# Expert activations turned by VectorE in 32 by 32 squares instead of by TensorE

## What is computed

```python
def expert_choice_ffn(h, w_router, w_gate, w_up, w_down):
    B, S, D = h.shape
    T = B * S
    xt = h.reshape(T, D)
    aff = jax.nn.softmax(jnp.einsum('td,de->te', xt, w_router).astype(jnp.float32), axis=-1)
    cap = CAPACITY_FACTOR * T // N_EXPERTS
    g, idx = lax.top_k(aff.T, cap)
    xe = xt[idx]
    hid = jax.nn.silu(jnp.einsum('ecd,edf->ecf', xe, w_gate)) * jnp.einsum('ecd,edf->ecf', xe, w_up)
    ye = jnp.einsum('ecf,efd->ecd', hid, w_down) * g[..., None].astype(h.dtype)
    out = jnp.zeros_like(xt).at[idx.reshape(-1)].add(ye.reshape(-1, D))
    return out.reshape(B, S, D)
```

## Time and profile before

| | us |
|---|---|
| median of 3 runs | 2111.11 |
| lowest, highest | 2111.06, 2111.87 |
| profiled execution | 2112.38 |
| its span, first to last instruction | 2110.5 |
| TensorE busy in the span | 1996.5 (95%) |
| VectorE, ScalarE, GpSimd busy | 399.8, 289.6, 138.5 |
| mean granted TensorE clock | 0.978 of full speed |
| moved by DMA | 639 MB, mean 303 GB/s |

### The profile page before, as it was taken

How to read it: one execution, slowest core, us unless ns; L and a number is a source line. 1 busy time by engine, 2 the same in 40 slices (tenths; PEclk the granted TensorE clock), 3 DMA queues, 4 the chain that set the end, 5 groups by cost and what they waited for, 6 DMA issues and landing times.

```text
span 2110.5 us, 37578 instructions
## 1 busy us (share of the span) xinstructions
PE 1996.5 (95%) x17115; PEld 921.3 (44%) x17115; DVE 399.8 (19%) x745; ACT 289.6 (14%) x556; POOL 138.5 (7%) x197
## 2 busy tenths in 40 slices
PE   6999999999957999999999999999999999999993
PEld 3888777776742333333333333333333333333331
DVE  1432255544360000010000100001000001000002
ACT  4222244442210000000000000000000000000001
POOL 1000000000100000010000100000000000100003
PEclk9999999999968999999999999999999999999997
DMA  9651111113059999999999999999999999999963
GB/s 381 234 203 58 33 56 50 41 51 130 30 213 374 393 395 413 389 385 408 389 411 389 399 393 389 410 391 407 395 381 413 388 412 389 381 412 389 414 222 106
DMA packets 101816, 639.19 MB, mean 303 GB/s; under 512 B 11489, under 2 KB 14945, under 8 KB 44065
## 3 DMA queue, kind: packets, MB, share of 16 engines
q1 hardware_dynamic: 95120, 620.32, 73.5%
q0 software_dynamic: 6544, 16.52, 3.7%
HBM read 622.90 MB, written 13.89 MB: 302 GB/s over the span
## 4 chain that ended last, share of the span: by engine, by line
PE 91%; DVE 3%; DMA 2%; ACT 2%; issue 1%; POOL 1%; SPq 0%; POOLq 0%; DVEq 0%; ACTq 0%
PE ps L738 87%; DMA slab_x<-in_w_mod_blocks 1%; PE ps L1122 1%; PE ps L907 1%; DVE negm L1614 1%; PE ps L1167 1%; PE ps L1125 0%; DMA xe<-xn_dram,idx_g 0%; DVE gq_lo L1586 0%; DVE in_lo L1538 0%; ACT in_hi L1233 0%; ACT gq_hi L1287 0%; DVE topi L1751 0%; PE ps L1038 0%; PE ps L826 0%
## 5 line engine op out<-in xcount | busy, mean ns | idle before, releaser
L738 PE MATMUL ps<-ring,xeT 128*32 128x512 f32 (+1 forms) x9216 | 927.2, 558 | 5.3 <-DVE hid L1832 3.3
L738 PEld LDWEIGHTS ps<-ring,xeT 128*32 128x32 f32 x9216 | 293.8, 110 | 601.7 <-issue 595.3
L738 PE MATMUL ps<-ring,hidT 128*32 128x512 f32 x4224 | 465.1, 592 | 0.9 <-ACT hidT L1442 0.9
L738 PEld LDWEIGHTS ps<-ring,hidT 128*32 128x32 f32 x4224 | 135.8, 110 | 305.2 <-issue 302.8
L1832 DVE TENSOR_TENSOR hid<-sil,ps 128x768 f32<-128x768 f32 (+1 forms) x48 | 42.6, 888 | 816.4 <-ACT sil L1437 816.4
L1437 ACT ACTIVATE sil<-ps 128x768 f32<-128x768 f32 (+1 forms) x48 | 36.3, 757 | 760.2 <-PE ps L738 760.2
L738 PE MATMUL ps<-in_hi,hT_hi 128*128 128x384 f32 x240 | 84.6, 353 | 12.5 <-DVE in_lo L1538 10.0
L738 PE MATMUL ps<-hT_hi,gq_hi 128*128 128x320 f32 x256 | 87.8, 343 | 0.0
L1442 ACT ACTIVATE hidT<-ps 128x384 f32<-128x384 f32 x48 | 23.5, 490 | 454.8 <-PE ps L1125 228.9
L738 PE MATMUL ps<-in_hi,hT_lo 128*128 128x384 f32 x240 | 82.3, 343 | 0.0
L738 PE MATMUL ps<-in_lo,hT_hi 128*128 128x384 f32 x240 | 82.1, 342 | 0.0
(11 more groups left out here) (211 smaller groups left out, 1377.8 us busy)
## 6 DMA issues: line engine op xcount, KB each, us to landing
ring<-in_w_gu SPq DMA_DIRECT2D x256, 1024.0 KB, 8.3
ring<-in_w_dn SPq DMA_DIRECT2D x176, 1024.0 KB, 8.2
ring<-in_w_gu_rest SPq DMA_DIRECT2D x128, 768.0 KB, 7.3
slab_y<-in_w_mod_blocks SPq DMA_DIRECT2D x8, 2048.0 KB, 8.6
in_slab<-in_w_in_blocks SPq DMA_DIRECT2D x6, 1536.0 KB, 9.0
gq<-in_w_gates SPq DMA_DIRECT2D x16, 512.0 KB, 3.5
slab<-in_w_mod_blocks SPq DMA_DIRECT2D x3, 2048.0 KB, 16.7
x<-in_x_sample SPq DMA_DIRECT2D x8, 512.0 KB, 11.0
```

What stands on the lines that cost most here:

```text
L738: return pe.matmul(out, lhsT, rhs, start=first, stop=last, **kw)
```

## The change

`hid` is turned by VectorE itself, straight from SBUF to SBUF, in one instruction for each group: `dve.transpose` turns each square of 32 partitions by 32 columns on its own. The squares stay where they are, so partition `32*x + j` of column block `c` now holds inner column `x*GW[G] + 32*c + j` of the group. The rows of the down weights are laid out on the host in that order, and the rest of the gate and up weights (G = 2) in four strips of 192 columns instead of 128 and 64. Sizes and number of all weight loads stay the same. `hid_T`, `turned_first`, `turned_second`, `inner` and their semaphores go; `hidT_ready` takes the place of `hidT_a` and `hidT_v`, and `gated` waits for it instead of `hidT_done`.

```diff
-    rest = [both[..., 2048:2560].reshape(2, E_, KD, P, 4, 128), both[..., 2560:].reshape(2, E_, KD, P, 4, 64)]
-    rest = np.concatenate(rest, 5).transpose(1, 2, 3, 4, 0, 5)
+    rest = both[..., 2048:].reshape(2, E_, KD, P, 4, 192).transpose(1, 2, 3, 4, 0, 5)
...
-    pairs = np.asarray(w_down)[0].reshape(E_, NF // 2, 2, P, D).transpose(0, 1, 3, 2, 4)
+    w, blocks, r = np.asarray(w_down)[0], [], 0
+    for n in GW:
+        blocks.append(w[:, r:r + 4 * n].reshape(E_, 4, n // 32, 32, D).transpose(0, 2, 1, 3, 4).reshape(E_, n // 32, P, D))
+        r += 4 * n
+    pairs = np.concatenate(blocks, 1).reshape(E_, NF // 2, 2, P, D).transpose(0, 1, 3, 2, 4)
...
-        hidT = [at(f"hidT{i}", E0 + 17408 + i * 3072, [P, 2, 3 * P]) for i in range(NGRP)]
+        hidT = [at(f"hidT{i}", E0 + 17408 + i * 3072, [P, 3, GW[i]]) for i in range(NGRP)]
...
                     last.then_inc(w_used, 1)
-                    if k == 0 and G > 0:
-                        hid_T(e, G - 1)
-                    elif k == 0 and not is_first(e):
-                        hid_T(before(e), NGRP - 1)
...
-                pe.wait_ge(hidT_a, val(e, NGRP, G + 1))
-                pe.wait_ge(hidT_v, val(e, NGRP, G + 1))
+                pe.wait_ge(hidT_ready, val(e, NGRP, G + 1))
...
-                            mm(ps[32 * x:32 * x + 32, 3, :], inner(G, c + i, x % 2), w[:, h0:h0 + 512],
+                            mm(ps[32 * x:32 * x + 32, 3, :], hidT[G][:, x % 2, 32 * (c + i):32 * (c + i) + 32], w[:, h0:h0 + 512],
...
                 multiply_expert((0, e))
-            hid_T((0, E_ - 1), 2)
             down((0, E_ - 1), 2)
...
-                    dve.wait_ge(hidT_done, val(e, NGRP, G))
+                    dve.wait_ge(hidT_ready, val(e, NGRP, G))
...
+            def turned(e, G):
+
+                dve.wait_ge(hid_ready, val(e, NGRP, G + 1))
+                dve.transpose(hidT[G][:, :, :], hid[:, :, 0:GW[G]]).then_inc(hidT_ready, 1)
...
             def expert_vector(e):
 
-                if not is_first(e):
-                    turned_second(before(e), 2)
                 gated(e, 0)
+                turned(e, 0)
                 if not is_first(e):
                     result_sum(before(e))
-                turned_second(e, 0)
                 gated(e, 1)
-                turned_second(e, 1)
+                turned(e, 1)
                 gated(e, 2)
+                turned(e, 2)
                 if not is_last(e):
                     tokens_scaled(after(e))
                     tokens_shifted(after(e))
```

More of the change, by code:

```diff
@@ L329, in program @@
         w_used = sem("w_used")
-        hidT_a, hidT_v = sem("hidT_a"), sem("hidT_v")
+        hidT_ready = sem("hidT_ready")
         tab_ready, tabT_done, tab_set = sem("tab_ready"), sem("tabT_done"), sem("tab_set")
@@ L337, in program @@
         pool_turn = sem("pool_turn")
-        xeT_done, sil_ready, hid_ready, hidT_done, yr_ready = (
-            sem(n) for n in ("xeT_done", "sil_ready", "hid_ready", "hidT_done", "yr_ready"))
+        xeT_done, sil_ready, hid_ready, yr_ready = (
+            sem(n) for n in ("xeT_done", "sil_ready", "hid_ready", "yr_ready"))
         gg2_done, gg2_ev, f_sq, f_ready, out_stored = (
@@ L1153, in down @@
                             h0 = i * D + x // 2 * 512
-                            mm(ps[32 * x:32 * x + 32, 3, :], inner(G, c + i, x % 2), w[:, h0:h0 + 512],
+                            mm(ps[32 * x:32 * x + 32, 3, :], hidT[G][:, x % 2, 32 * (c + i):32 * (c + i) + 32], w[:, h0:h0 + 512],
                                first and i == 0, last_ and i == 1)
                     for x in range(4):
-                        last = mm(ps[32 * x:32 * x + 32, 4, :], inner(G, c + x // 2, 2), w[:, x * 512:x * 512 + 512],
-                                  first, last_)
+                        last = mm(ps[32 * x:32 * x + 32, 4, :], hidT[G][:, 2, 32 * (c + x // 2):32 * (c + x // 2) + 32],
+                                  w[:, x * 512:x * 512 + 512], first, last_)
                     last.then_inc(w_used, 1)
@@ L1437, in silu @@
                 act.activation(sil[:, :, 0:GW[G]], ps[:, 0:3, 0:GW[G]], ACT.Silu).then_inc(sil_ready, 1)
-            def turned_first(e, G):
-                act.wait_ge(hidT_done, val(e, NGRP, G + 1))
-                act.activation(hidT[G][:, 0, :], ps[:, 5, 0:3 * P], ACT.Copy).then_inc(hidT_a, 1)
             def result_out(e):
@@ L1452, in expert_scalar @@
             def expert_scalar(e):
-                if not is_first(e):
-                    turned_first(before(e), 2)
                 silu(e, 0)
@@ L1458, in expert_scalar @@
                     result_out(before(e))
-                turned_first(e, 0)
                 silu(e, 1)
-                turned_first(e, 1)
                 silu(e, 2)
@@ L1468, in _ @@
             expert_scalar((0, E_ - 1))
-            turned_first((0, E_ - 1), 2)
             result_out((0, E_ - 1))
@@ L1878, in _ @@
             expert_vector((0, E_ - 1))
-            turned_second((0, E_ - 1), 2)
             result_sum((0, E_ - 1))
```

## The result

The changed kernel takes 2057.23 us (median of 4 runs, 2056.57 to 2058.11) against 2111.49 us; the ratio is 0.9741, with a 95% interval from 0.9730 to 0.9753.

What follows compares the result with a forecast made beforehand. The prediction took TensorE as the bound, the DMA close under it: turns free 51.4 us, but meeting the DMA late leaves a gain of 44.7; 2112.4 less that is 2067.7, median 1.3 lower, so 2066 us, range 2058 to 2078.

## What to carry to other kernels

Where two engines are both busy all the time, find the bound by who waits; then price the other by making the first one faster, not by its busy share, since packets in a short queue take longer than they need. A prefetch ring turns a head start into time: as long as lead is left, the faster engine's pace holds although the slower one could not keep it up. And take durations from start to start when you multiply them by hundreds.

## What the runs showed of the hardware

- VectorE turns 128 x 768 floats in squares of 32 in 0.98 us and 128 x 576 in 0.78.
- One core's loads ran at 419 GB/s for tens of microseconds, and at the DMA's own pace an expert's 34.6 MB, gather and scatter took 86.4 us, 400 GB/s for the weights alone.
- A scatter beside a short queue of loads pressed the DMA to 165 GB/s for 3 us; beside loads in line the 9 us of its dip ran at 388 and 377.
- In the changed kernel the stream ran at about 213 GB/s with a share of 0.51 from 1987 us to 1996 and ended at 1999; in the kernel before, where no long line had formed, it went from full rate to nothing in some 2 us. Why half of the engines' work ends later isn't shown.
- Pauses of TensorE of 2 us (7 of 15 in one run) and 3.3 us (in 4 of 14 traces) were followed by 3.4 or 6.8 us at half the granted clock.
- TensorE waited 9.7 to 10.1 us for a gather issued behind 14 loads of 1 MiB, and 5.2 to 5.3 us behind 10 or 8.
